# Order of work between and inside the feed-forwards of a two-layer encoder: when weights are split, finished blocks added, squares summed

## The chip, the cores and the metric

One NeuronCore of a Trainium2 chip runs the whole program. The metric is device microseconds from launch to end, the median of several executions. An engine is named as the profile names it: PE (TensorE, matrix products), PEld (its weight loads), DVE (VectorE), ACT (ScalarE), POOL (GpSimd) and SP (SyncE, which here only issues transfers).

## What is computed

The input x is 512 tokens of 1024 features in float32. There are two layers, and each is

```
x = x + 0.5 * swiglu(rms(x, ffn1_norm), ffn1_w)      # feed-forward, 2816 hidden columns
x = x + mixer(rms(x, mix_norm))                      # layer 0: windowed attention, layer 1: latent attention
x = x + 0.5 * swiglu(rms(x, ffn2_norm), ffn2_w)
swiglu(h, w) = (silu(h @ w_gate) * (h @ w_up)) @ w_down
```

and a last rms norm. So four feed-forwards run one after the other, numbered f = 0 to 3 here; mixers stand between 0 and 1 and between 2 and 3, and nothing stands between 1 and 2.

## The kernel before

**Numbers.** PE multiplies rounded float32 values. To keep precision each operand is split in two: ACT copies it into a rounded high part, DVE subtracts that from the original and leaves the low part. A product is then three matmuls (high by high, high by low, low by high). Every weight goes through ACT and then DVE before PE can use it; `high...` functions are ACT's half of a split and `low...` functions DVE's half.

**Units.** A feed-forward is 30 units, u = 0 to 29 (`ffn_units`, line 50): 22 "G" units (one gate and up tile of 128 hidden columns each) and 8 "D" units (blocks of the down projection, put in after unit 9 and after the second run of gates). A unit of 2 by 2 blocks is done with seven products instead of eight, in the way of Strassen and Winograd: weights are combined into sums, inputs are combined into sums, and the results are combined again. Product q of unit u is P_q(u) below: 12 matmuls of 256 columns. Unit 0 is done without this, as two plain tiles of 48 matmuls (`plain_tile`, line 1895). PE's order is in `ffn` at line 1922: in period u it runs P1(u), P2(u), P4(u-1), P6(u), P3(u-1), P5(u), P7(u). P4 and P6 add to a bank that holds an earlier product, so they wait until that has been copied out.

**Weights.** Each unit has six splits, called fills (`fill`, line 555): FA (1024 columns), FB, FC, FD, FE and FU (512 each). FB holds the sum called S2 and feeds P6, FE feeds P7, FU P5, FC P4, FD P3, and FA both P1 and P2. FU, FB and FD of one unit come out of one buffer, a chain of four: SP loads a first piece, and POOL adds three more pieces by accumulating transfers (`link`, line 775). Step 0 makes FU's data; when FU has been split, step 1 adds a piece and makes FB's; when FB has been split, step 2 makes FD's. FE comes from a single buffer with one added piece (`join`, line 790). FA and FC are loaded plain. POOL's order of issues is in `ffn` at line 798.

**Order on ACT and DVE.** Both run in program order (ACT: `ffn`, line 994; DVE: `ffn`, line 1465), and a wait of one item holds up all behind it. In period u ACT does: FU(u+1), copy of P1 (line 1005, "first copy"), FA(u+1), silu of the first half, FC(u), copy of P6 (line 1021), FB(u+1), FD(u), silu of the second half of u-1, copy of P7 (line 1042, "last copy"), FE(u+1). P4(u) in the next period waits for that last copy. DVE has the low halves in the same order, with the sums and products of results among them: addition with the last copy at line 1541, norm factor of the gate at line 1422. `fill_count` (line 74) gives each fill its place in this order; semaphores fill_hi and fill_lo are waited on by these counts, so the count and the two engines' orders must be the same.

**Combined units.** In units 3, 5, 7, 9, 14, 17, 19 and 21 (`combined`, line 169) the hidden columns just computed are combined into the inputs of the down projection as well: DVE makes four sums (line 1246 to 1254), and ACT and DVE split seven blocks of 256 columns (lines 904, 913, 1259, 1269).

**Between feed-forwards.** The output of what came before f = 1, 2, 3 (8 blocks of 128 features) is added to x in `pairs_out` (ACT line 954, DVE line 1340). Per block j, DVE first splits the weights of block n+j+3 (`low`), then adds block j to x (line 1351); ACT scales the new x (line 925), squares it (line 937), and per pair of blocks the split inputs and sums of the first products are made (`pair_split`, `pair_mix`). Fills FA, FU and FC of unit 0 stand at j = 6, at j = 7 and after the loop. Then `begin` makes FU(1), the last mixed inputs, the norm (POOL's power, line 773, and four small steps on DVE), FA(1), FB(1) and FE(1). For f = 0 the inputs come from transposes, and squares and sums alternate with the mixed inputs (lines 1075 and 1596). `sums` (line 1956) adds the squares over features on PE; `spread` (line 1968) puts the norm factor on all partitions.

**Transfers that the end of a feed-forward waits for.** In f = 0 and 2 SP loads rotary tables before it loads the first blocks of what follows, and waits for the last FE to be split (line 696); ACT's first `high` of those blocks stands in unit 29 (line 1008), DVE's at line 1499.

```python
                if part is not None:
                    sp.wait_ge(fill_lo, fill_count(f, FE, NU - 1))
                    sp.dma_start(tables[:, part * S:3 * S], consts[:, P + part * S:]).then_inc(t_in, 16)
```

## Time and profile before

| | us |
|---|---|
| median of 3 runs (lowest, highest) | 1857.53 (1855.23, 1859.74) |
| the profiled execution, its own time | 1855.27 |
| its span, first to last instruction | 1853.5 |
| PE busy | 1737.3 |
| DVE busy | 1417.2 |
| ACT busy | 954.8 |
| mean granted TensorE clock | 0.981 |

The profile is of one execution. A row of a timeline is: start in us, duration in us, engine, line of the kernel, operation, tile written, tiles read, shape, number of instructions merged, and in brackets the idle time of the engine before it with what ended it. The arrow points to what was waited for. PEclk is the TensorE clock granted, as a share of full speed.

### The profile page before, as it was taken

How to read it: one execution, taken by the hardware profiler on the slowest of the kernel's cores; microseconds unless marked ns; L12 is line 12 of the kernel's file. 1: busy time of each engine (PE TensorE's matmuls, PEld its weight loads, DVE VectorE, ACT ScalarE, POOL GpSimd, SP SyncE). 2: the span in 40 equal slices, each digit the busy share in tenths (PEclk: the TensorE clock that was granted, in tenths of full speed). 3: DMA queues.
4: the chain of work that ended last, by engine and by line, in shares of the span. 5: the costliest groups of instructions: out<-in, count | busy, mean ns of one | idle time of the engine just before them, and what ended most of it. 6: DMA issues, size and time to landing. Idle time of an engine off the chain costs nothing. (4 is left out here: it accounts for less than half of the span.)

```text
span 1853.5 us, 34651 instructions
## 1 busy us (share of the span) xinstructions
PE 1737.3 (94%) x12937; PEld 1626.4 (88%) x12937; DVE 1417.2 (76%) x2776; ACT 954.8 (52%) x1892; POOL 434.8 (23%) x495
## 2 busy tenths in 40 slices
PE   5999999999989999999799999999999889999997
PEld 4999999877879899998799999987867789999995
DVE  5788787667678878866778788766897568878788
ACT  4554554446555545544555455544565445555452
POOL 0333333111013333330133333300000033333320
PEclk7999999999989999999899999999999989999999
DMA  5899999533439999995399999945112389999971
GB/s 173 192 219 237 224 220 229 149 110 91 125 91 220 221 228 217 226 245 154 69 224 224 226 223 230 209 117 132 30 40 58 108 182 220 230 226 221 226 163 69
DMA packets 187076, 324.18 MB, mean 175 GB/s; under 512 B 24545, under 2 KB 58526, under 8 KB 186910
## 3 DMA queue, kind: packets, MB, share of 16 engines
q0 software_dynamic: 66816, 121.66, 38.5%
q1 hardware_dynamic: 118528, 198.55, 33.9%
q8 instruction: 105, 1.72, 0.4%
q10 hardware_dynamic: 1566, 1.74, 0.3%
q14 instruction: 61, 0.50, 0.1%
HBM read 315.33 MB, written 2.10 MB: 171 GB/s over the span
## 5 line engine op out<-in xcount | busy, mean ns | idle before, releaser
L1889 PE MATMUL bank<-h_all,w_all 128*128 128x256 f32 x2352 | 672.2, 286 | 45.0 <-ACT work L1042 34.0
L1890 PE MATMUL bank<-h_all,w_all 128*128 128x256 f32 x2352 | 668.2, 284 | 0.0
L1891 PE MATMUL bank<-h_all,w_all 128*128 128x256 f32 x2352 | 668.0, 284 | 0.0
L1889 PEld LDWEIGHTS bank<-h_all,w_all 128*128 128x128 f32 x2352 | 453.9, 193 | 52.4 <-issue 34.4
L1890 PEld LDWEIGHTS bank<-h_all,w_all 128*128 128x128 f32 x2352 | 454.1, 193 | 0.0
L1891 PEld LDWEIGHTS bank<-h_all,w_all 128*128 128x128 f32 x2352 | 453.9, 193 | 0.0
L787 POOL DMA_DIRECT2D work<-ffn_gu x252 | 221.6, 923 | 825.3 <-DVE w_all L1238 593.3
L901 ACT ACTIVATE w_all<-work 128x512 fp32r<-128x512 f32 x352 | 208.9, 623 | 345.6 <-DMA work<-ffn_gu 222.3
L1238 DVE TENSOR_TENSOR w_all<-work,w_all 128x512 fp32r<-128x512 f32 x352 | 238.9, 687 | 150.4 <-ACT w_all L901 149.6
L1238 DVE TENSOR_TENSOR w_all<-r_all,w_all 128x512 fp32r<-128x512 f32 (+1 forms) x356 | 308.2, 866 | 21.7 <-ACT w_all L901 16.9
L901 ACT ACTIVATE w_all<-r_all 128x512 fp32r<-128x512 f32 (+1 forms) x356 | 273.0, 769 | 73.3 <-PE bank L1891 71.9
L1889 PE MATMUL bank<-y_all,w_all 128*128 128x256 f32 x896 | 254.4, 284 | 11.8 <-DVE w_all L1238 11.2
L1890 PE MATMUL bank<-y_all,w_all 128*128 128x256 f32 x896 | 253.7, 283 | 0.0
L1891 PE MATMUL bank<-y_all,w_all 128*128 128x256 f32 x896 | 253.6, 283 | 0.0
L1889 PEld LDWEIGHTS bank<-y_all,w_all 128*128 128x128 f32 x896 | 172.0, 192 | 13.3 <-DVE w_all L1238 13.3
L1891 PEld LDWEIGHTS bank<-y_all,w_all 128*128 128x128 f32 x896 | 172.0, 192 | 0.0
L1890 PEld LDWEIGHTS bank<-y_all,w_all 128*128 128x128 f32 x896 | 172.0, 192 | 0.0
L992 ACT ACTIVATE work<-work 128x256 f32<-128x256 f32 x168 | 70.0, 417 | 142.1 <-DVE work L1422 141.8
L787 POOL DMA_DIRECT2D work<-ffn_d x96 | 87.1, 991 | 165.0 <-DVE w_all L1238 165.0
L1225 DVE TENSOR_TENSOR w_all<-x_f,w_all 128x1024 fp32r<-128x1024 f32 (+2 forms) x72 | 69.0, 959 | 61.4 <-ACT w_all L876 55.9
L1409 DVE SCALAR_TENSOR_TENSOR xT<-bank,xT 128x256 f32<-128x256 f32 x224 | 93.9, 419 | 22.9 <-PE bank L1891 21.6
L1842 PE MATMUL bank<-y_all,w_all 128*128 128x512 f32 x272 | 107.4, 395 | 1.3 <-DVE w_all L1225 1.3
(214 smaller groups left out, 2787.1 us busy)
## 6 DMA issues: line engine op xcount, KB each, us to landing
work<-ffn_gu POOLq DMA_DIRECT2D x252, 256.0 KB, 5.9
r_all<-ffn_gu SPq DMA_DIRECT2D x88, 512.0 KB, 5.2
r_all<-ffn_gu SPq DMA_DIRECT2D x172, 256.0 KB, 6.3
work<-ffn_d POOLq DMA_DIRECT2D x96, 256.0 KB, 6.1
work<-ffn_gu SPq DMA_DIRECT2D x88, 256.0 KB, 5.6
r_all<-ffn_gu POOLq DMA_DIRECT2D x84, 256.0 KB, 7.2
r_all<-ffn_d SPq DMA_DIRECT2D x64, 256.0 KB, 5.8
r_all<-ffn_d SPq DMA_DIRECT2D x32, 512.0 KB, 5.3
```

The costliest lines, as they stand in the source:

```text
L787: pool.dma_start(chain[g % CHAIN], unit_source(f, u, slice(part * S, (part + 1) * S)), accum_op=ALU.add).then_inc(chain_sum[g % CHAIN], 16)
L901: a.activation(hi, src, ACT.Copy).then_inc(fill_hi, 1)
L992: a.activation(buf, buf, ACT.Silu).then_inc(silu_done, 1)
L1225: last = v.tensor_tensor(w_lo[:, sl, 0:k, 0:m], w_raw[:, sl, 0:k, 0:m], w_hi[:, sl, 0:k, 0:m].bitcast(F32), ALU.subtract)
L1238: v.tensor_tensor(lo, src, hi.bitcast(F32), ALU.subtract).then_inc(fill_lo, 1)
L1409: return v.scalar_tensor_tensor(at, src, -0.5 if c < PAIRED else 0.5, at, ALU.mult, ALU.add)
L1842: t.matmul(b[:, :], wh, hi[:, c, :], start=c == 0, stop=False)
L1889: t.matmul(o, wh, xh, start=c == 0 and not on, stop=False, skip_group_check=on)
L1890: t.matmul(o, wh, xl, start=False, stop=False, skip_group_check=on)
L1891: last = t.matmul(o, wl, xh, start=False, stop=c == PAIRED - 1, skip_group_check=on)
```

## The change

Six things are reordered. No instruction is added or taken away, and no transfer changes its size.

1. FB(u) and FE(u) are split in period u and no longer in period u-1. FB(u) comes first in the period, FE(u) after the first copy on ACT and after the norm of the gate on DVE (for u > 1).
2. In period u the silu of the second half comes before FD(u) on ACT. On DVE the addition after the last copy (`finish`) moves to the start of the next period, ahead of FB. In the units of f = 3 that also transpose x, it thereby comes after those transposes.
3. POOL's loop is written in another order to match.
4. `pairs_out`: DVE adds block j to x first and then splits the weights of block n+j+4; fills FA, FU, FC of unit 0 move to j = 4, 5, 6, and FU(1) to the end of the loop. The inputs of the last pair are split and mixed at j = 7 and right behind it.
5. f = 0: all squares and their sums come before any mixed input.
6. f = 0: PE runs both plain tiles before `sums`, and P2(1) before `spread`.

In the diff, the functions `ffn` come in the order POOL, ACT, DVE, PE; `pairs_out` is DVE's, and ACT's is changed alike. `finish(f, u)` and `finish_late(f, u)` hold the additions that stood at the end of period u.

```diff
 def fill_count(f, kind, u):
     if u < 2:
-        at = {FA: 0, FU: 1, FC: 2}[kind] if u == 0 else {FU: 3, FA: 4, FB: 5, FE: 6, FC: 9, FD: 11}[kind]
-    elif u == NU - 1 and kind in (FC, FD):
-        at = 6 * NU - (5 if kind == FC else 4)
+        at = {FA: 0, FU: 1, FC: 2}[kind] if u == 0 else {FU: 3, FA: 4, FB: 5, FE: 6, FC: 9, FD: 10}[kind]
+    elif kind in (FU, FA):
+        at = (7 if kind == FU else 8) if u == 2 else 6 * u - (6 if kind == FU else 4)
     else:
-        at = 6 * u + {FU: -5, FA: -4, FB: -2, FE: 0, FC: 3, FD: 5}[kind]
+        at = 6 * u - 1 + {FB: 0, FE: 2, FC: 4, FD: 5}[kind]
+        if u == NU - 1 and kind != FB:
+            at -= 1 if kind == FE else 2
...
             def ffn(f, m):
-                for u in range(NU + 1):
+                for u in range(NU):
+                    if u > 0:
+                        link(f, u, 2)
                     link(f, u + 1, 1)
                     if u == 0:
                         power(m)
                     link(f, u + 2, 0)
                     join(f, u + 2)
-                    link(f, u + 1, 2)
...
             def ffn(f):
+                    if u > 1:
+                        high_fill(f, FB, u)
                     high_fill(f, FU, u + 1)
...
+                    if u > 1:
+                        high_fill(f, FE, u)
                     high_fill(f, FA, u + 1)
...
-                    high_fill(f, FB, u + 1)
+                    if before:
+                        silu(f, u - 1, 1)
                     high_fill(f, FD, u)
                     if u == NU - 1:
                         high(SEG_AT[f] + 1, end)
-                    if before:
-                        silu(f, u - 1, 1)
...
-                    high_fill(f, FE, u + 1)
...
             def pairs_out(n, f, factor, begun=0):
                 end = n + KD
+                if not begun:
+                    low(n + AHEAD, end)
                 for j in range(KD):
-                    if j >= begun:
-                        low(n + j + AHEAD, end)
-                    if j == KD - 2:
-                        low_fill(f, FA, 0)
-                    if j == KD - 1:
-                        low_fill(f, FU, 0)
                     b = product(n + j)
                     v.scalar_tensor_tensor(xT[:, PERM[j], :], b[:, :], factor, xT[:, PERM[j], :],
                                            ALU.mult, ALU.add).then_inc(evac_done, 1)
-                    if j >= 3 and j % 2 and j < KD - 1:
-                        q = (j - 3) // 2
-                        low_mixed(h_mix, combine_count(f, q, False), q)
+                    low(n + j + AHEAD + 1, end)
+                    if 4 <= j < 7:
+                        low_fill(f, (FA, FU, FC)[j - 4], 0)
                     if j >= 2 and j % 2 == 0:
-                        pair_split(f, j // 2 - 1)
-                        pair_mix(f, j // 2 - 1)
+                        low_mixed(h_mix, combine_count(f, j // 2 - 1, False), j // 2 - 1)
                     if j:
                         added(j == 1)
-                pair_split(f, PAIRED - 1)
+                    if j % 2:
+                        pair_split(f, j // 2)
+                        if j < KD - 1:
+                            pair_mix(f, j // 2)
                 added(False)
-                low_fill(f, FC, 0)
-                low_mixed(h_mix, combine_count(f, PAIRED - 2, False), PAIRED - 2)
                 pair_mix(f, PAIRED - 1)
+                low_fill(f, FU, 1)
...
             def ffn(f, m):
+                    if u > 1:
+                        finish(f, u - 1)
+                        low_fill(f, FB, u)
                     low_fill(f, FU, u + 1)
+                    if u > 1 and UNITS[u - 1][0] == "D":
+                        finish_late(f, u - 1)
...
+                    if u > 1:
+                        low_fill(f, FE, u)
                     low_fill(f, FA, u + 1)
...
-                    low_fill(f, FB, u + 1)
...
             for k in range(KD):
                 added(k == 0)
-                if k % 2:
-                    pair_mix(0, k // 2)
-                    if k < KD - 1:
-                        low_mixed(h_mix, combine_count(0, k // 2, False), k // 2)
...
             def ffn(f, m, ready):
                 plain_tile(f, False)
-                sums(m, KD)
+                if f > 0:
+                    sums(m, KD)
                 plain_tile(f, True)
                 if f > 0:
                     pe.wait_ge(evac_done, ready)
+                else:
+                    sums(m, KD)
                 product(f, 1, 1)
-                spread(m + 1)
-                for q in (2, 6, 5, 7):
+                if f > 0:
+                    spread(m + 1)
+                product(f, 2, 1)
+                if f == 0:
+                    spread(m + 1)
+                for q in (6, 5, 7):
                     product(f, q, 1)
```

## Rows read from the trace of the kernel before

**Rows 1.** Who PE waited for: us in total, times, longest.
```profile
PE bank L1889 <- ACT work L1042: 34.0, 30, 3.3
...
PE bank L1964 <- DVE acc L1286: 14.7, 1, 14.7
PE bank L1916 <- DVE y_all L1264: 13.4, 5, 4.8
```

**Rows 2.** Windows: units without a stall; all four feed-forwards from P1(1) on.
```profile
655.00:725.00 70.00, 70.00 (x586) 70.00 (x585) 53.12 (x102) 35.64 (x63) 23.55 (x27) 1.00 1.02 234
...
sum 1245.50, PE 1188.74 PEld 1179.75 DVE 985.30 ACT 653.08 POOL 388.68; mean PE 297.19 PEld 294.94 DVE 246.33 ACT 163.27 POOL 97.17
```

**Rows 3.** Windows: the way into f = 1, and the start of f = 0.
```profile
526.00:549.00 23.00, 16.23 (x106) 16.06 (x107) 15.84 (x27) 8.93 (x14) 4.11 (x4) 0.78 0.26 66
...
32.80:50.00 17.20, 6.51 (x30) 6.51 (x31) 13.10 (x24) 7.32 (x11) 4.14 (x4) 0.50 0.10 17
```

**Rows 4.** Timeline of PE, into f = 1: last block, P1(1), P7(1).
```profile
525.49 0.39 PE L1844 MATMUL bank<-y_all,w_all 128*128 128x512 f32 x1
...
548.87 0.28 PE L1889 MATMUL bank<-h_all,w_all 128*128 128x256 f32 x1
...
556.62 0.36 PE L1889 MATMUL bank<-h_all,w_all 128*128 128x256 f32 x1 [1.37 <-DVE w_all L1238]
```

**Rows 5.** Timeline of DVE, into f = 1: last block added, last pair split, FU(1).
```profile
533.49 0.68 DVE L1351 SCALAR_TENSOR_TENSOR xT<-bank,xT 128x512 f32<-128x512 f32 x1
...
536.78 0.42 DVE L1264 TENSOR_TENSOR y_all<-work,y_all 128x256 fp32r<-128x256 f32 x1
...
541.10 0.68 DVE L1238 TENSOR_TENSOR w_all<-work,w_all 128x512 fp32r<-128x512 f32 x1
```

**Rows 6.** Timeline of POOL, into f = 1: step 0 of unit 2, issued behind the power.
```profile
544.40 0.90 POOL L787 DMA_DIRECT2D work<-ffn_gu  x1
```

**Rows 7.** Timeline of ACT, into f = 1: FU(2) when step 0 has landed.
```profile
551.14 0.63 ACT L901 ACTIVATE w_all<-work 128x512 fp32r<-128x512 f32 x1 [1.01 <-DMA work<-ffn_gu]
```

**Rows 8.** Timeline of DVE: FU(1) of f = 2 and of f = 3.
```profile
910.75 0.68 DVE L1238 TENSOR_TENSOR w_all<-work,w_all 128x512 fp32r<-128x512 f32 x1
...
1488.77 0.69 DVE L1238 TENSOR_TENSOR w_all<-work,w_all 128x512 fp32r<-128x512 f32 x1
```

**Rows 9.** Timelines at f = 0: DVE's first split of mixed inputs; PE's sums and P7(1).
```profile
30.28 1.23 DVE L1269 TENSOR_TENSOR h_all<-work,h_all 128x1024 fp32r<-128x1024 f32 x1 [1.12 <-ACT h_all L913]
...
43.49 0.37 PE L1964 MATMUL bank<-ones,acc 128*128 128x1 f32 x1 [14.65 <-DVE acc L1286]
...
60.88 0.36 PE L1889 MATMUL bank<-h_all,w_all 128*128 128x256 f32 x1 [1.42 <-DVE w_all L1238]
```

**Rows 10.** Timelines, combined unit 7 of f = 1: ACT's FB and last copy, DVE, PE's P4(7).
```profile
622.57 1.15 ACT L901 ACTIVATE w_all<-work 128x512 fp32r<-128x512 f32 x2 [3.16 <-DMA work<-ffn_gu]
...
625.57 0.36 ACT L1042 ACTIVATE work<-bank 128x256 f32<-128x256 f32 x1
...
621.56 0.95 DVE L1259 TENSOR_TENSOR y_all<-work,y_all 128x768 fp32r<-128x768 f32 x1
...
626.08 0.36 PE L1889 MATMUL bank<-h_all,w_all 128*128 128x256 f32 x1 [1.50 <-ACT work L1042]
```

**Rows 11.** Timelines, unit 29 of f = 2: DVE's FE(29), its gate norm; ACT's first next block.
```profile
1212.44 0.69 DVE L1238 TENSOR_TENSOR w_all<-r_all,w_all 128x512 fp32r<-128x512 f32 x1
...
1215.52 0.42 DVE L1422 TENSOR_TENSOR work<-work,r_x 128x256 f32<-128x256 f32 x1
...
1218.45 0.85 ACT L876 ACTIVATE w_all<-x_f 128x768 fp32r<-128x768 f32 x1 [5.12 <-DMA x_f<-ffn_e]
```

**Rows 12.** The source view: joins (line 795) idle until; landing of joins, then of links (line 787).
```profile
  issue: 162.3, 86
...
DMA to landing us min/median/max: 4.8/6.9/9.8
...
DMA to landing us min/median/max: 3.5/6.0/10.9
```

More of the change, by code:

```diff
@@ L1077, in _ @@
                 squared(xT[:, PERM[j], :], j == 0)
-                if j % 2 and j < KD - 1:
-                    high_mixed(h_mix, combine_count(0, j // 2, False), j // 2)
             end = SEG_AT[1]
@@ L1342, in pairs_out @@
                 end = n + KD
+                if not begun:
+                    low(n + AHEAD, end)
                 for j in range(KD):
[L1344 to L1349 removed]
                     b = product(n + j)
```

69 lines of the change are left out of this document (42 added, 27 removed).

## The prediction

> **What bounds the kernel.** I read who PE waited for first. PE is busy for 1737.3 of 1853.5 us, so the end is set by PE's own work and by its stalls, and only a stall taken away moves it. Of the stalls, the largest single one in number is the last copy on ACT, 34.0 us in 30 waits; 14.7 us is one wait for the sums of squares at the start; 13.4 us is for the inputs of the plain tiles [rows 1]. Then windows. In 70 us without a stall PE starts 586 matmuls, one per 0.1195 us, so that a product (12) takes 1.43 us and a period of seven 10.04 us. From P1(1) to the end each of the four feed-forwards is 203 products or 291 us; together 1166 us, while they took 1245.5 us [rows 2]. So 79 us are stalls inside, beside those on the ways in. On the way into f = 1 PE is busy for 16.2 of 23 us, at 0.78 of its clock, and DVE for 15.8: neither is full, which is the sign of a chain in which each waits for the other [rows 3].
>
> **Part 4, the ways in (f = 1, 2, 3).** The last block before f = 1 leaves PE at 525.9, P1(1) starts at 548.87 and P7(1) at 556.62 [rows 4]. What lies between is 96 matmuls of the plain tiles (11.5 us) and the sums (0.5), so P1(1) could stand at 537.9. It doesn't, because block 7 is added to x only at 533.49, 7.6 us after PE had it: DVE stands in front of it with FA and FU of unit 0, which wait for ACT, which waits for DVE's block before. From that add to the last split of the pair is 3.7 us, and from there to the end of the split FU(1) another 4.6, at 541.8 [rows 5]. With the add first, block 7 is added at 526.0. The pair is split at 529.7, before the first tile's last quarter (525.9 and 4.3), and FU(1), now ahead of the last mixed split of 1.2 us that stood before it and of FC, is done near 532.4: 9.4 earlier. FU(1) is the start of what follows: POOL issues step 1 of unit 1, then the power, then step 0 of unit 2 at 544.40 [rows 6]; that lands and lets ACT do FU(2) at 551.14 [rows 7], and the first copy, which P6(1) needs, stands behind FU(2). All of this moves along by 9.4 with unchanged lengths. PE is ahead of it (P2(1) ends near 541.3, FU(2) comes at 541.8), so the late thing is then step 0 of unit 2, and P6(1) waits 1.6 us for it. I take **-9.4** for f = 1. Bounds: 11.0 (P1(1) alone would move so much) and 4.0, if DVE is so far behind at j = 7 that only half is had.
>
> For f = 3 the same: FU(1) was done at 1489.5 [rows 8], the last block leaves PE at 1472.4 (the same distance of 6.4 us gives 1478.9), **-10.5**. For f = 2 a block is 18 matmuls of 512 columns, near 4.1 us, and DVE's work on one (a split, an add, half a pair) is near 4.3, so DVE is about 4 us late at block 7. FU(1), done at 911.4 before, comes at 902.5: **-8.9**. SP's and POOL's first loads of the next feed-forward are not behind any of this. Low and high splits of blocks n+4 to n+7 come at most one add (0.68) later for PE, which needs them three blocks later: nothing. If that cover were gone, it would be 0.7 for each of 5 blocks.
>
> **Parts 5 and 6, f = 0.** Sums came at 43.49 after an idle time of 14.65 us, since each round had a mixed input, in which DVE waited 1.12 for ACT [rows 9]. Seven adds back to back at 0.79 each from 26.95 end at 32.4, and PE meanwhile does the second tile, to 34.5. But the four mixed inputs now come after: for each DVE three sums (1.6), ACT's half (1.1), DVE's half (1.2), 3.9 in all with the waits, from 34.1 to 50.1 with the norm between. P6(1) needs all four, and ACT's first copy is behind the last of them, near 51. PE thus idles from about 41 to 51, and its restart is at half the clock as the first one was (0.50 from 32.8 to 50 [rows 3]). The silu and the copies of unit 1 then set P7(1), near 57.2 in place of 60.88 [rows 9]: **-3.7**. Bounds: -6 and +2 (if a slow restart pushes P6(1) past those copies). The Trainium skill, TensorE: Matmul & The Clock Gate, HAM oscillation, says the same of a wait as this row, that work after it starts cold; were the restart warm, P6 and P5 would end 2.9 earlier and P7(1) would still wait for the copy, so the sum would not change.
>
> **Parts 1 and 2, inside.** In unit 7 ACT sat idle 3.16 us until FB(8) had landed, and behind it stood FD(7), the silu, a mixed input and the last copy, at 625.57. P4(7) waited 1.50 for that [rows 10]. With FB behind the copy, a plain unit's P4 no longer waits. A combined unit keeps DVE's own chain: its split of 621.56 ends at 622.5, then the norm (0.4), silu (0.5), FD (0.5), mixed (0.9), copy (0.4): 625.2 less overlaps of a few tenths, 0.8 us sooner. Of the 34.0 us some 5.6 belong to unit 29 (below). The other 28.4, in 26 waits, lose 0.8 each, 20.8. Against it, FB is now split by DVE after that late copy, and P6 wants it 4.3 us into the period; after a combined unit I get 4.7 to 5.1, a wait of 0.3 in 24 places, 7. **-14**. Bounds: -34, all of that row and nothing given back, and 0, all given back.
>
> **POOL.** The sequence of issues is the same as before, only the loop is written differently: step 2, step 1, step 0, join. The times differ. The join waited for nothing that a semaphore tells for 162.3 us in 86 cases, and landings take 6.0 us for a link and 6.9 for a join [rows 12]; the spacing fits three such transfers in flight at most, the fourth issued when one lands. Steps 2 and 1 are now 0.6 us apart instead of 3 to 5, so step 0 has to wait for the join of the unit before, near 5.8 us into a period. It lands 2.4 into the next, where FU wants it at 1.1. There are 1.9 us left before the first copy makes P6 late: nothing, unless landings grow. **The 16 DMA engines** are 1.02 busy at 234 GB/s at full speed [rows 2], and one unit is nine pieces of 256 KB, 10.1 us at that rate; three units are loaded ahead, so 27 in 294 us need 272. I exclude a bound by bytes.
>
> **The end of f = 0 and 2.** Here the change costs. SP's loads of the next blocks wait for FE(29), which was split at 1212.44 and now comes after the gate's norm, which ends at 1215.9 [rows 11]: 3.5 us later. ACT already sat idle 5.12 us for such a load at 1218.45, with the silu, FC(29) and the P6 copy behind it, so P7(29) and P4(29) are 3.5 later. And silu, FD(29), the next block and the last copy are now in a row after the silu: 1.4 more. **+4.9** each, 9.8. For f = 1 and 3, whose loads are early, 1.5 each: **+3**. Bounds: +6 and +16.
>
> **Sum.** -9.4 -10.5 -8.9 -3.7 -14 +9.8 +3 = -33.7 us. Against the profiled execution, 1855.3, that is 1821.6. The median of the runs stands 2.3 above it, 1857.5, and for the median I say 1824. A difference under 0.2% (3.7 us) can't be told from none here.
>
> **Rivals.**
> (a) DVE is the bound. It is busy 53.1 of 70 us [rows 2], but in a combined unit its list is about 11 us against a period of 10. Then what P4 gains P6 gives back (0 for -14), and the ways in give half (-16 for -32.5). With +12.8 that is -3, or 1854; with the ways in full, -20, or 1838. For it: the 0.3 above is a difference of large numbers. Against it: each other unit leaves 2 us to catch up. Chance 0.19 for something from 1838 to 1852.
> (b) Slower: POOL's three places. From FB(u) to FU(u+3) there is now a chain of three landings (step 2, join, step 0), 19 us of landing and 1 of issue, in 20.1 + 1.4. If bunched transfers land 15% later, 22 us, the excess is 1.5 in each two periods, over 116 periods 87 us, less -34 with the stalls inside: about +40, or 1897. It decides once the three take over 20.7. Maxima of 9.8 and 10.9 are in the rows [rows 12], but in crowds at a start. For the crowding: the Trainium skill, DMA: Bandwidth & Descriptors, Issuing engines are not separate DMA queues, says that all queues share the same 16 engines and interleave. By that, spacing within a period changes no total, and rows 2 agree, with 1.02 busy and PE still full. Chance 0.07.
> (c) No change, losses at the end of a feed-forward and the gains cancelling: 0.04.
> (d) As computed, 1808 to 1838: 0.66. More than that, stalls inside nearly all gone: 0.04.
> That gives faster 0.89, same 0.04, slower 0.07. The range for 8 in 10 takes (d) and the better half of (a): 1804 to 1848.
>
> **What would show it.** Into f = 1, block 7 is added within 1 us of PE's end of it, and P1(1) starts within 14 us of it. The wait for the last copy falls under 20 us. POOL's idle before its links moves to step 0. At the end of f = 0 and 2, ACT waits over 7 us for the next block. I am wrong if PE waits for FB in every period, if FU waits over 3 us for its landing in steady units, or if DVE has no idle time left before f = 1.

## The result: 0.85% slower, and the profile after

The changed kernel takes 1874.07 us (median of 4 runs, 1865.85 to 1876.89) against 1856.38 us before (4 runs). The ratio is 1.0085, with a 95% interval from 1.0059 to 1.0111. Forecast were 1824 us and 0.982.

| | before | after |
|---|---|---|
| the profiled execution, its own time, us | 1855.27 | 1865.85 |
| span, us | 1853.5 | 1864.0 |
| PE, DVE, ACT busy, us | 1737.3, 1417.2, 954.8 | 1745.0, 1420.5, 953.5 |
| mean granted TensorE clock | 0.981 | 0.984 |

The profiled execution was the shortest of the four. So the sum of the prediction is judged against a difference of 10.6 us in span; what the other three took on top has no trace.

The next table cuts both spans at starts and ends of products on PE. "Inside" is P7(1) to P1(28), "end" is P1(28) to the end of P3(29), "way" is from there to the next P7(1).

| stretch, us | before | after | difference | forecast |
|---|---|---|---|---|
| start to P7(1) of f = 0 | 60.9 | 55.5 | -5.4 | -3.7 |
| ways into f = 1, 2, 3 | 194.1, 66.3, 277.3 | 194.5, 57.1, 275.7 | +0.4, -9.2, -1.6 | -9.4, -8.9, -10.5 |
| inside f = 0, 1, 2, 3 | 274.8, 277.6, 275.5, 278.3 | 282.6, 279.6, 279.9, 281.6 | +17.4 together | -14 |
| ends of f = 0, 1, 2, 3 | 26.8, 25.1, 25.8, 25.7 | 32.1, 24.1, 28.7, 31.0 | +5.3, -1.0, +2.9, +5.3 | +4.9, +1.5, +4.9, +1.5 |
| after the last P3(29) | 45.2 | 41.5 | -3.7 | 0 |

Two rows are far off: the ways into f = 1 and 3, and inside. The waits of PE after the change, to be set beside [rows 1] (us in total, times, longest):

```profile
PE bank L1911 <- ACT work L1052: 30.2, 27, 2.9
PE bank L1911 <- DVE w_all L1245: 27.3, 33, 9.6
PE bank L1938 <- DVE y_all L1271: 22.6, 8, 6.4
...
PE bank L1911 <- ACT work L1014: 4.5, 7, 2.5
```

The wait for the last copy (now line 1052) fell only from 34.0 to 30.2. Waits for splits of weights (line 1245), which cost 14.8 us before, take 27.3 (9.6 of it is one wait at the start of f = 0, below), those of the plain tiles for their inputs (line 1271) 22.6 in place of 13.4, and PE now waits for the first copy (line 1014).

**The way into f = 1.** Timelines of ACT, of DVE and of PE (start, us, engine, line; in brackets idle time before it):

```profile
527.78 1.06 ACT L904 ACTIVATE w_all<-r_all 128x1024 fp32r<-128x1024 f32 x1 [9.03 <-PE bank L1866]
...
533.23 0.63 ACT L904 ACTIVATE w_all<-work 128x512 fp32r<-128x512 f32 x1 [2.30 <-PE bank L1866]
```

```profile
520.76 0.68 DVE L1354 SCALAR_TENSOR_TENSOR xT<-bank,xT 128x512 f32<-128x512 f32 x1
...
531.76 0.68 DVE L1354 SCALAR_TENSOR_TENSOR xT<-bank,xT 128x512 f32<-128x512 f32 x1
...
538.18 0.68 DVE L1354 SCALAR_TENSOR_TENSOR xT<-bank,xT 128x512 f32<-128x512 f32 x1
...
541.13 0.69 DVE L1354 SCALAR_TENSOR_TENSOR xT<-bank,xT 128x512 f32<-128x512 f32 x1
```

```profile
544.99 0.56 PE L1938 MATMUL bank<-h_all,w_all 128*128 128x256 f32 x1 [6.43 <-DVE y_all L1271]
```

Blocks 4 to 7 are added at 520.76, 531.76, 538.18 and 541.13. PE had the last of them at 533.13, so block 7 is added 8.0 us late, where it was 7.6 before [rows 4, 5]. Between blocks 4 and 5 stand 11 us: ACT waits 9.03 us to split FA of unit 0, and what it waits for is a matmul of the block products. FA goes into slot 0 of `w_all`, FU into slot 1, FC into slot 2. The eight blocks lie in slots 2, 3, 0, 1, 2, 3, 0, 1 for f = 1 and 3, and in 0, 1, 2, 3, 0, 1, 2, 3 for f = 2 (`slot`, `high_fill`). So at j = 4 FA waits for PE's block 6, and at j = 5 FU for block 7; at j = 6 ACT had split FA before the change without a wait:

```profile
525.61 1.04 ACT L901 ACTIVATE w_all<-r_all 128x1024 fp32r<-128x1024 f32 x1
```

In f = 2, where FA and FU wait for blocks 4 and 5, the way is 9.2 us shorter, near the 8.9 forecast.

**Inside.** Stalls of PE between P7(1) and P1(28), by the product that they precede, summed over four feed-forwards (distance of two starts less 12 times 0.1197 us, 183 distances in each):

| us before | P1 | P2 | P3 | P4 | P5 | P6 | P7 | all |
|---|---|---|---|---|---|---|---|---|
| kernel before | 0.6 | 0.4 | 2.2 | 32.7 | 0.6 | 17.9 | 0.4 | 54.8 |
| after | 1.1 | 5.6 | 4.6 | 26.9 | 0.4 | 31.2 | 2.6 | 72.3 |

P4 gained 5.8 and everything else lost 23. And P4 gained in plain units only: in the 32 combined units its stalls are 27.3 us before and 26.7 after, in all others 5.4 before and 0.2 after. Of P6's 31.2 us, 19.0 stand in the units that follow a combined one and 6.9 in the combined ones. Two of ACT's waits, first before and then after the change (us in total, times, longest):

```profile
ACT work L992 <- DVE work L1422: 141.8, 148, 3.2
```

```profile
ACT work L999 <- DVE work L1438: 322.3, 146, 5.4
```

ACT's waits for landings of the links' data fell from 337.4 us to 163.7, and those for DVE's norm of the gate rose by 180.5: the idle time changed its cause and did not go. Combined unit 7 of f = 1 after the change, to be set beside [rows 10]; timelines of ACT, DVE and PE:

```profile
631.74 0.42 ACT L999 ACTIVATE work<-work 128x256 f32<-128x256 f32 x1 [4.07 <-DVE work L1438]
632.06 0.61 ACT L904 ACTIVATE w_all<-work 128x512 fp32r<-128x512 f32 x1
632.58 1.04 ACT L916 ACTIVATE y_all<-work 128x1024 fp32r<-128x1024 f32 x1
633.53 0.36 ACT L1052 ACTIVATE work<-bank 128x256 f32<-128x256 f32 x1
```

```profile
631.29 0.42 DVE L1438 TENSOR_TENSOR work<-work,r_x 128x256 f32<-128x256 f32 x1
632.71 0.69 DVE L1245 TENSOR_TENSOR w_all<-work,w_all 128x512 fp32r<-128x512 f32 x1 [1.00 <-ACT w_all L904]
```

```profile
634.04 0.36 PE L1911 MATMUL bank<-h_all,w_all 128*128 128x256 f32 x1 [1.25 <-ACT work L1052]
```

ACT no longer waits for the landing of FB. It waits 4.07 us for DVE's norm of the gate instead, then come silu, FD, mixed inputs and at last the copy for P4(7), which stalls 1.25 us where it stalled 1.50. And DVE now stands still for 1.00 us between its norm and its half of FD, because on ACT the silu is ahead of FD.

**Ends.** ACT's first block of what follows in f = 0 and f = 2, to be set beside the 5.12 us of [rows 11]:

```profile
358.78 0.84 ACT L879 ACTIVATE w_all<-x_f 128x768 fp32r<-128x768 f32 x1 [8.10 <-DMA x_f<-ffn_e]
...
1224.45 0.84 ACT L879 ACTIVATE w_all<-x_f 128x768 fp32r<-128x768 f32 x1 [6.31 <-DMA x_f<-ffn_e]
```

In f = 3 it is another thing, two transposes of x (line 1420) that now stand ahead of DVE's addition and of FB(29). Timelines of DVE and PE:

```profile
1803.83 2.50 DVE L1420 STREAM_TRANSPOSE x_f<-xT 32x1024 f32<-32x1024 f32 x2
1806.36 0.42 DVE L1487 TENSOR_TENSOR work<-bank,work 128x256 f32<-128x256 f32 x1
```

```profile
1807.43 0.38 PE L1911 MATMUL bank<-h_all,w_all 128*128 128x256 f32 x1 [1.39 <-DVE w_all L1245]
...
1819.62 0.55 PE L1911 MATMUL bank<-h_all,w_all 128*128 128x256 f32 x1 [1.70 <-DVE work L1487]
```

PE loses 5.3 us there, but the kernel does not: from P1(29) to the end DVE is the later engine (its last transposes end at 1840.73, and 23.3 us of final norm follow the last transposes in both kernels), so that end and tail together cost 1.6.

**The start of f = 0.** A window while P6(1) waits, and PE's wait:

```profile
41.47:50.46 8.99, 0.00 (x1) 0.02 (x1) 6.54 (x11) 4.04 (x7) 0.00 (x0) 0.50 0.30 50
```

```profile
50.46 0.57 PE L1911 MATMUL bank<-h_all,w_all 128*128 128x256 f32 x1 [9.58 <-DVE w_all L1245]
```

PE idles for 9 us, with a granted clock of 0.50, as the prediction had it (41 to 51), and P7(1) comes at 55.5.

### The profile page after: what moved, and what is told of

The parts are those of the page before. It is cut to its first block and busy times, and to the rows that moved or that the text cites. A ratio compares the mean times of both kernels' runs of the same rounds, so it can differ in the third digit from the quotient of the medians.

```text
span 1864.0 us, 34651 instructions
## 1 busy us (share of the span) xinstructions
PE 1745.0 (94%) x12937; PEld 1627.1 (87%) x12937; DVE 1420.5 (76%) x2776; ACT 953.5 (51%) x1892; POOL 436.5 (23%) x495
## 5 line engine op out<-in xcount | busy, mean ns | idle before, releaser
L1911 PE MATMUL bank<-h_all,w_all 128*128 128x256 f32 x2352 | 676.9, 288 | 60.8 <-ACT work L1052 30.2
L904 ACT ACTIVATE w_all<-work 128x512 fp32r<-128x512 f32 x352 | 215.7, 624 | 213.8 <-DMA work<-ffn_gu 102.3
L1245 DVE TENSOR_TENSOR w_all<-r_all,w_all 128x512 fp32r<-128x512 f32 (+1 forms) x356 | 299.1, 864 | 12.8 <-ACT w_all L904 12.1
L904 ACT ACTIVATE w_all<-r_all 128x512 fp32r<-128x512 f32 (+1 forms) x356 | 264.3, 767 | 48.9 <-PE bank L1913 32.6
L1864 PE MATMUL bank<-y_all,w_all 128*128 128x512 f32 x272 | 107.1, 394 | 0.0
L1866 PE MATMUL bank<-y_all,w_all 128*128 128x512 f32 x272 | 106.1, 390 | 0.0
```

The lines of the kernel that those rows point to most:

```text
L904: a.activation(hi, src, ACT.Copy).then_inc(fill_hi, 1)
L1245: v.tensor_tensor(lo, src, hi.bitcast(F32), ALU.subtract).then_inc(fill_lo, 1)
L1864: t.matmul(b[:, :], wh, hi[:, c, :], start=c == 0, stop=False)
L1866: last = t.matmul(b[:, :], wl, hi[:, c, :], start=False, stop=c == k - 1)
L1911: t.matmul(o, wh, xh, start=c == 0 and not on, stop=False, skip_group_check=on)
```

## The experiments

Two bases are used: the changed kernel (runs a_...), and the kernel before with parts 4 to 6 alone (b_...); a_part1 and the runs p1_... are the latter with part 1 added. Stalls are those inside, as in the table above; for the changed kernel 72.3 us. The expectations count about 11.9 us more in each such total (5.8 at P5 and 5.8 at P6, which the starts in the traces don't bear out). It is the same amount in every run, so differences between runs stand, and a bound of theirs is compared after taking 11.9 off a total and 5.8 off P6.

| run | median, us | ratio to before, 95% interval | stalls inside | span of the profile |
|---|---|---|---|---|
| a_slots | 1862.67 | 1.0023 (1.0001 to 1.0044) | 88.5 | 1862.8 |
| a_fd_first | 1857.28 | 0.9998 (0.9978 to 1.0018) | 68.0 | 1855.9 |
| a_tables_late | 1868.11 | 1.0037 (1.0015 to 1.0059) | 90.0 | 1872.5 |
| a_fd_copy1 | 1856.79 | 0.9991 (0.9968 to 1.0014) | 62.8 | 1845.8 |
| a_nojoin | 1868.40 | 1.0044 (1.0029 to 1.0059) | 70.4 | 1867.0 |
| a_pool_sum | 1895.56 | 1.0197 (1.0162 to 1.0231) | 100.4 | 1897.7 |
| b_outer | 1838.86 | 0.9892 (0.9856 to 0.9928) | 46.0 | 1832.8 |
| b_outer_slots | 1828.56 | 0.9826 (0.9788 to 0.9864) | 54.6 | 1827.2 |
| b_copy_early | 1828.10 | 0.9822 (0.9791 to 0.9853) | 58.0 | 1825.6 |
| b_pool_sum | 1836.39 | 0.9897 (0.9866 to 0.9927) | 61.6 | 1831.7 |
| b_best | 1835.05 | 0.9877 (0.9857 to 0.9898) | 67.6 | 1833.8 |
| a_part1 | 1857.57 | 1.0002 (0.9979 to 1.0024) | 82.5 | 1853.5 |
| b_light | 1814.28 | 0.9772 (0.9739 to 0.9804) | 42.1 | 1810.4 |
| p1_light | 1823.45 | 0.9824 (0.9779 to 0.9870) | 45.3 | 1816.0 |
| p1_nostep2 | 1819.46 | 0.9790 (0.9759 to 0.9820) | 46.2 | 1820.3 |
| b_nostep2 | 1801.46 | 0.9688 (0.9658 to 0.9718) | 30.7 | 1799.5 |
| b_copy_tables | 1823.82 | 0.9806 (0.9781 to 0.9832) | 56.9 | 1822.1 |

How far one profile can be trusted: f = 0 is the same code in the changed kernel, a_slots and (up to its end) a_tables_late, and took 282.6, 285.5 and 285.5 us inside. So a few us of one stretch are not told apart by single profiles; medians and ratios decide where they disagree. a_nojoin, b_light, p1_light and the two runs without step 2 leave work out, so their outputs are not those of the program: they measure, and are no versions to use.

**1. Slots (a_slots).** FILL_AT is 6 for f = 1 and 3, and 4 for f = 2; ACT's side is edited alike.

```diff
-                    if 4 <= j < 7:
-                        low_fill(f, (FA, FU, FC)[j - 4], 0)
+                    if FILL_AT[f] <= j < FILL_AT[f] + 3:
+                        low_fill(f, (FA, FU, FC)[j - FILL_AT[f]], 0)
...
+                if FILL_AT[f] == 6:
+                    low_fill(f, FC, 0)
```

> The changed kernel, but on the ways into f = 1 and 3 fills FA, FU and FC of unit 0 stand at j = 6, at j = 7 and after the loop again (behind the addition of the block), as the slots of w_all that they need come free there; the way into f = 2 keeps j = 4, 5, 6. Theory 1 (slots): in f = 1 and 3 FA at j = 4 has to wait for PE's block 6 and FU at j = 5 for block 7, and the additions of blocks 5 to 7 stand behind them. Then the way into f = 1 (end of P3(29) to P7(1), 194.5 us in the changed kernel) falls to 185 to 187 and into f = 3 (275.7) to 266 to 269, the rest stays, the span falls from 1864 to 1846 to 1849. Rival (DVE simply has too much work on these ways, wherever the fills stand): each way gets at most 2 shorter, span 1860 or more.

The ways came out as expected: 184.3 us into f = 1 and 266.5 into f = 3, so 10.2 and 9.2 shorter. DVE's addition of block 7, and the window from PE's end of block 7 to P1(1), in this run:

```profile
536.58 0.69 DVE L1357 SCALAR_TENSOR_TENSOR xT<-bank,xT 128x512 f32<-128x512 f32 x1 [0.38 <-PE bank L1871]
```

```profile
536.20:548.78 12.58, 12.58 (x107) 12.54 (x105) 10.00 (x20) 7.23 (x11) 4.12 (x4) 1.00 0.20 37
```

DVE waits for PE and not the other way round. From the end of block 7 to P1(1) PE is busy throughout, for 12.6 us in place of 23, and the clock stays at 1.00, where it was 0.78 [rows 3]. But the span fell by 1.2 only, to 1862.8, which is what the rival had (1860 or more), since stalls inside grew by 16 in this profile. By the medians the gain is 11.4. The mechanism is shown by the ways; the 15 to 18 us expected to the end of the kernel were not had.

**2. FD ahead of the silu (a_fd_first).**

```diff
-                    if before:
-                        silu(f, u - 1, 1)
                     high_fill(f, FD, u)
                     if u == NU - 1:
                         high(SEG_AT[f] + 1, end)
+                    if before:
+                        silu(f, u - 1, 1)
```

> The changed kernel, but in each period ACT splits FD(u) before the silu of the second half, as before the change. Theory 2 (a round trip): with the silu first DVE stands still 1.00 us in every period between the norm of the gate and its half of FD, and in combined units, where DVE is the bound, that pushes the last copy and all that follows. Then DVE's idle time in front of fills from work for ACT (176 us) falls by 50 to 100, the stalls of P4 in combined units (1.41 each) fall to 0.4 to 0.9, the stalls between P7(1) and P1(28), 84 us in all, to 60 to 72, and the span to 1842 to 1852. Rival (FB at the head of the period is what costs, or POOL's landings): under 4 us in all, stalls in front of P6 unchanged.

P4's stalls fell from 26.9 to 13.3, and the one that recurs in combined units (5, 7 and 19 above all) from 1.41 to 0.89, as expected; P6's grew from 31.2 to 39.3, and neither the stalls inside (expected 48 to 60 by this count) nor the span (1842 to 1852) got where theory 2 had them. The timeline of DVE in unit 7 shows where the 1.00 us went, and ACT's shows who is late now:

```profile
628.13 0.68 DVE L1245 TENSOR_TENSOR w_all<-work,w_all 128x512 fp32r<-128x512 f32 x1
629.65 1.23 DVE L1276 TENSOR_TENSOR y_all<-work,y_all 128x1024 fp32r<-128x1024 f32 x1 [0.83 <-ACT y_all L916]
```

```profile
625.48 0.63 ACT L904 ACTIVATE w_all<-work 128x512 fp32r<-128x512 f32 x1 [1.30 <-DMA work<-ffn_gu]
```

FD follows the norm without a wait, but then DVE waits 0.83 us for the mixed inputs, and ACT waits 1.30 for the landing of FD's data. The median fell by 16.8 and the span by 8.1, of which f = 3's end and tail are 3.7 and the stalls inside 4.3. Theory 2 is half right: the round trip is real, its removal is partly given back.

**3. Parts 4 to 6 alone (b_outer, b_outer_slots).**

> The kernel before with parts 4, 5 and 6 alone (additions first on the ways in, squares ahead of sums at f = 0), order inside the units as before. If the parts add up: f = 0 starts 5.4 us earlier, the ways give 0 (f = 1), 9.2 (f = 2), 1.6 (f = 3), the stalls inside and the ends are those of before: span 1836 to 1840 against 1853.5. If the gains on the ways hang on the order inside the units (what POOL and SP issue first, and so the landings), the sum is under 10 us: 1844 or more.

> The kernel before with parts 4, 5 and 6 and with the fills of unit 0 where their slots are free (j = 6, 7, end for f = 1 and 3, j = 4, 5, 6 for f = 2). By theory 1 and the sum of the run before: 16 us more than that, span 1819 to 1824. By the rival of theory 1 no better than 1835.

b_outer is 1.1% faster than before, a little more than the parts summed to (span 1832.8 against 1836 to 1840). With the fills where their slots are free it is 1.7% faster. The ways are 7.8 and 7.7 us shorter than in b_outer, but of these 15.5 the median shows 10.3 and the span 5.6 (1827.2, outside the expected 1819 to 1824): P4's stalls inside rose from 26.2 to 33.3. So parts 4 to 6 are a gain even as they stand in the change, and the loss lies in parts 1 to 3.

**4. SP's wait ahead of the tables (a_tables_late).**

```diff
-                if part is not None:
-                    sp.wait_ge(fill_lo, fill_count(f, FE, NU - 1))
-                    sp.dma_start(tables[:, part * S:3 * S], consts[:, P + part * S:]).then_inc(t_in, 16)
                 for j in range(KD):
+                    if part is not None and j == SLOTS:
+                        sp.wait_ge(fill_lo, fill_count(f, FE, NU - 1))
+                        sp.dma_start(tables[:, part * S:3 * S], consts[:, P + part * S:]).then_inc(t_in, 16)
```

> The changed kernel, but at the end of f = 0 and f = 2 SP issues the loads of the next four blocks ahead of its wait for FE(29) and the load of the tables. Theory 3 (the step of the prediction on the ends): FE(29) is split 3.5 us later than before the change, and behind that wait stand the loads of the next blocks, for which ACT waits. Then the end of f = 0 (P1(28) to the end of P3(29), 32.1 us in the changed kernel) falls to 25 to 27 and that of f = 2 (28.7) to 25 to 26.5, the span by 8 to 10 us. Rival (the order silu, FD, next block inside unit 29 is what lengthens the ends): they fall by under 2 us each, the span by under 4.

The end of f = 0 fell from 32.1 to 24.1 and that of f = 2 from 28.7 to 25.0. ACT's first block in f = 0 no longer waits for a landing:

```profile
355.15 0.85 ACT L879 ACTIVATE w_all<-x_f 128x768 fp32r<-128x768 f32 x1 [0.60 <-PE bank L1913]
```

Theory 3 holds for the stretch. The span of this profile is longer all the same (stalls inside 90.0); the median is 6.0 lower, with intervals that just touch (1.0015 to 1.0059, and 1.0059 to 1.0111 for the changed kernel).

**5. The two copies moved on ACT (a_fd_copy1, b_copy_early).** In the first the first copy goes ahead of FU(u+1), in the second the last copy ahead of the mixed inputs:

```diff
+                    if gate and u > 1:
+                        act.wait_ge(prod_done, product_count(f, 1, u))
+                        act.wait_ge(e_2, at)
+                        a.activation(s_1, b[:, 0:HN], ACT.Copy).then_inc(e_1, 1)
                     high_fill(f, FU, u + 1)
```

```diff
+                    if gate:
+                        act.wait_ge(prod_done, product_count(f, 7, u))
+                        act.wait_ge(e_5, at)
+                        a.activation(u_3, b[:, 0:HN], ACT.Copy).then_inc(e_7, 1)
                     if q is not None:
                         high_mixed(y_mix, combine_count(f, q, True), q % PAIRED)
```

> The run with FD ahead of the silu, and ACT's first copy ahead of FU(u+1) too (from u = 2 on). Theory 4 (a queue on ACT): with FB(u) and FU(u+1) both at the head of the period, the first copy, which P6(u) needs, stands behind FU(u+1), whose data land late; PE waited 14.2 us for it in 17 places. Then these waits go, the stalls in front of P6 (45 us) fall to 31 to 35, the span (1855.9) to 1843 to 1848. Rival (DVE's fills are late anyway, so that P6 waits for FB in the same places): P6's stalls stay over 40 and the span over 1852.

> The kernel before with parts 4 to 6 and the fills where their slots are free, and ACT's last copy ahead of the split of the mixed inputs in combined units (1.04 us of work of ACT moved behind it). If the last copy is only late by what stands ahead of it on ACT, the stalls of P4 in combined units fall by up to 1.04 each: P4's 33 us inside to 12 to 18, the span from 1827 to 1808 to 1814. Rival (DVE's own list bounds a combined unit, so that what P4 gains P6 or the next unit loses): total of the stalls inside falls by under 7 us, span 1820 or more.

(At the old places the same lines are taken out.) Both moved the stall that they were aimed at, and neither moved the time. Waits of PE for copies, first a_fd_first, then a_fd_copy1 (its last copy is line 1056):

```profile
PE bank L1911 <- ACT work L1014: 14.2, 17, 1.8
PE bank L1911 <- ACT work L1052: 12.6, 17, 1.7
```

```profile
PE bank L1915 <- ACT work L1056: 21.2, 20, 1.7
```

The 14.2 us for the first copy are gone, P6's stalls fell from 39.3 to 21.9, and P4's rose from 13.3 to 22.6. In b_copy_early P4's fell from 33.3 to 12.7 and P6's rose from 17.3 to 34.9. The medians went from 1857.3 to 1856.8 and from 1828.6 to 1828.1. (The profile of a_fd_copy1, 1845.8, was the shortest of its ten runs; by it alone theory 4 would look right.) This is what rival (a) of the prediction said: what P4 gains P6 gives back.

**6. Fewer transfers on POOL (a_nojoin).** The accumulating transfer for FE is left out.

> The changed kernel without POOL's adding transfer of the buffer of FE (its sum lacks one piece; 116 transfers of 256 KB fewer, a quarter of POOL's). If the stalls in front of P6 come from landings (POOL has at most three transfers in flight and the links stand bunched), the irregular ones go: P6 37 us to 18 to 24, DVE and ACT wait less for links, span 1845 to 1852. If they come from the order on DVE and ACT alone, P6's stalls stay over 32 and the span over 1858.

P6's stalls stayed (32.1 for 31.2), with ACT's waits for the links' data down from 102.3 us to these:

```profile
ACT w_all L902 <- DMA work<-ffn_gu: 77.7, 63, 4.8
```

The median is 5.7 lower, with intervals that just touch. The mere number of POOL's transfers is not what costs most.

**7. A sum on POOL (a_pool_sum, b_pool_sum), and with the tables' edit (b_best).**

```diff
+            def first_sum(f, q):
...
+                g.tensor_tensor(x_sum[:, 0:2, :], x[:, 2:0:-1, :], x[:, 3:4, :].to_broadcast([P, 2, HN]), ALU.subtract)
...
                     link(f, u + 1, 1)
+                    if u in COMBINED:
+                        first_sum(f, COMBINED[u])
                     link(f, u + 2, 0)
```

> The changed kernel, with the first of the four sums of a combined unit (0.69 us on DVE) made by POOL, between the issues of step 1 and step 0. Theory 5 (DVE bounds the combined units): a cycle of a combined and the next plain unit is 14 products, 20.1 us, but DVE is busy for 20.5 us in it; the cycle took 21.4 us before the change and 22.2 after it, the difference being DVE's own waits. Then 0.6 less work of DVE shortens each such cycle by 0.4 to 0.6: stalls inside 84 to 68 to 76, median (1874) down by 8 to 16 us. Rival (the waits for landings and the order on ACT bound the cycle): no more than 3 us.

> The same edit on the kernel before with parts 4 to 6 and the fills where their slots are free (median 1828.6, stalls inside 66.5 us). Theory 5: cycle from 21.5 to 20.9 or less, P4's stalls 33 to 20 to 25 with no growth at P6, median 1814 to 1820. Rival (as for the run before): 1825 or more.

> The run with the sum on POOL, and SP's loads of the next four blocks ahead of its wait for FE(29) and the tables. If theories 3 and 5 hold and add up: 3 to 4 us under the run with the sum alone (ends 26.9 and 25.9 to 24.1 and 25.0), median 1811 to 1816. If a faster end is given back on the way in or inside: no difference from it.

a_pool_sum is 21.5 us slower than the changed kernel, b_pool_sum and b_best are 7.8 and 6.5 slower than b_outer_slots (the last with intervals that overlap). DVE was not relieved. Groups of instructions by form, in b_outer_slots and in b_pool_sum (busy us, mean ns):

```profile
L1243 DVE TENSOR_TENSOR w_all<-r_all,w_all 128x1024 fp32r<-128x1024 f32 x120 | 146.3, 1219 | 9.4 <-ACT w_all L902 9.2
```

```profile
L1253 DVE TENSOR_TENSOR w_all<-r_all,w_all 128x1024 fp32r<-128x1024 f32 x120 | 178.8, 1490 | 8.4 <-ACT w_all L912 8.2
```

```profile
L804 POOL TENSOR_TENSOR work<-work 128x512 f32<-128x512 f32 x32 | 45.9, 1434 | 0.0
```

DVE's half of FA grew by 32.5 us over the kernel. In the trace 29 of its 120 instructions overlap a sum of POOL (1.43 us) and take 2.34 us in the mean, the other 91 take 1.22: 1.1 us more for each that overlaps, while the sum that left DVE was 0.69. On POOL the sum also waits for its inputs ahead of step 0, which was not measured by itself. So the test said nothing on theory 5, and the runs of the next part replace it. (The 20.5 us in the expectation is PE's mean busy time of a cycle; DVE's is 18.3, see the rows of the next part.)

**8. Which part, and by what (a_part1, b_light, p1_light, p1_nostep2, b_nostep2).** a_part1 is b_outer_slots with part 1 alone, and with the order of POOL's loop that belongs to it (part 3), so the two are not told apart:

> The kernel before with parts 4 to 6, free slots, and of the changes inside the units part 1 alone (FB(u) and FE(u) split in period u, POOL's order with it); the silu and DVE's addition after the last copy stand as before the change. It splits the loss inside: against the same kernel without part 1 (span 1827, stalls inside 66.5). Theory 6 (part 1 costs: FB and FU stand together at the head of a period, where ACT and DVE are late after the last copy, and DVE waits for ACT for each): stalls inside 76 to 84, with the later ends of f = 0 and 2 a span of 1840 to 1848. Rival (the silu and the moved addition were the cost): stalls inside 64 to 70, span 1831 to 1836, which is the ends alone.

It took 82.5 us of stalls inside, 27.9 more than b_outer_slots, and a median 29.0 higher, more than either theory had: part 1 by itself costs 1.8% of the kernel. Parts 1 and 2 together (a_slots) stand at 1.0023, part 1 at 1.0002, so the silu and the moved addition cost about 0.2%, where the two intervals overlap. That is less than a_fd_first gave for the silu alone in the changed kernel (from 1.0085 to 0.9998, 0.9%). No run explains the difference, so the price of part 2 is known only as 0.2 to 0.9%.

Then two remedies on both sides of part 1. "light" does four operations of DVE in combined units on 8 columns only, "nostep2" drops step 2 of the links:

```diff
-                        mix(q % 2, k, 0)
+                        mix(q % 2, k, 0, 8)
...
-                        normed_silu(f, u - 1, 0)
+                        normed_silu(f, u - 1, 0, 8 if u in COMBINED else HN)
```

```diff
-                    if u > 0:
-                        link(f, u, 2)
...
-    return 16 * (3 * CHAIN_TURN[f, u] + steps)
+    return 16 * (2 * CHAIN_TURN[f, u] + min(steps, 2))
```

> The kernel before with parts 4 to 6 and free slots (median 1828.6, stalls inside 66.5 us), where in combined units four of DVE's operations (the first sum, two norms of the gate, one of the silu) work on 8 columns only, so that sums and norms are left out there for the other columns: about 1.6 us less for DVE in each combined unit. Theory 5 (DVE's list bounds them): the cycle of a combined and a plain unit falls from 21.5 to 20.2 to 20.5 us, the stalls inside to 35 to 48, the span to 1796 to 1810. Rival (landings, or the order on ACT): stalls inside over 58, span over 1819.

> The same relief of DVE on the kernel with part 1 added (median 1857.6, stalls inside 94.4 us, cycle 22.2). If part 1 costs because DVE, already full, gets waits of its own at the head of a period, the cycle falls by 1.2 to 1.6 and the stalls inside to 50 to 66. If part 1 costs through landings, they stay over 75.

> The kernel with part 1, without step 2 of POOL's links (the data of FD lack a piece and are ready when FB's are; 116 transfers fewer). Landings as the cause of part 1's cost: ACT no longer waits for FD's data, the last copy is earlier, stalls inside 94.4 to under 78, median 1857.6 to under 1842. DVE or the order as the cause: stalls inside over 88, median over 1852.

> The kernel before with parts 4 to 6 and free slots (median 1828.6, stalls inside 66.5 us) without step 2 of POOL's links (FD's data lack a piece; 116 transfers fewer). If the late landing of step 2 is what part 1 brings, it costs next to nothing here: stalls inside 58 to 66, median 1820 to 1828, against a fall of 38 us for the same edit with part 1. If landings cost the same in both orders, the stalls inside fall under 45 and the median under 1808.

| ratio to before | as it is | light | no step 2 |
|---|---|---|---|
| without part 1 | 0.9826 | 0.9772 | 0.9688 |
| with part 1 | 1.0002 | 0.9824 | 0.9790 |
| cost of part 1 | 1.8% | 0.5% | 1.0% |

By the intervals of the ratios each cost is uncertain by 0.4 to 0.6 points (an estimate from their widths): with "light" it can't be told from none, and the fall from 1.8% to 1.0% is only just clear.

The cycle of a combined and the next plain unit (P4(3) to P4(5), P4(5) to P4(7), P4(7) to P4(9) and P4(19) to P4(21) of each feed-forward, 16 windows), summed; with the mean busy time of each engine. In turn: before, after, b_outer_slots, b_light, b_nostep2, a_part1, p1_light, p1_nostep2.

```profile
sum 342.37, PE 327.93 PEld 324.80 DVE 293.11 ACT 196.44 POOL 112.46; mean PE 20.50 PEld 20.30 DVE 18.32 ACT 12.28 POOL 7.03
```

```profile
sum 355.32, PE 334.11 PEld 325.15 DVE 295.13 ACT 196.19 POOL 112.38; mean PE 20.88 PEld 20.32 DVE 18.45 ACT 12.26 POOL 7.02
```

```profile
sum 343.73, PE 327.55 PEld 324.93 DVE 294.05 ACT 197.18 POOL 112.48; mean PE 20.47 PEld 20.31 DVE 18.38 ACT 12.32 POOL 7.03
```

```profile
sum 338.84, PE 326.34 PEld 323.40 DVE 271.87 ACT 195.75 POOL 112.63; mean PE 20.40 PEld 20.21 DVE 16.99 ACT 12.23 POOL 7.04
```

```profile
sum 335.53, PE 326.65 PEld 323.49 DVE 291.50 ACT 195.47 POOL 85.32; mean PE 20.42 PEld 20.22 DVE 18.22 ACT 12.22 POOL 5.33
```

```profile
sum 355.10, PE 334.14 PEld 325.07 DVE 294.31 ACT 200.09 POOL 112.32; mean PE 20.88 PEld 20.32 DVE 18.39 ACT 12.51 POOL 7.02
```

```profile
sum 334.98, PE 327.14 PEld 323.67 DVE 269.16 ACT 197.44 POOL 112.37; mean PE 20.45 PEld 20.23 DVE 16.82 ACT 12.34 POOL 7.02
```

```profile
sum 343.60, PE 331.98 PEld 324.47 DVE 292.58 ACT 195.78 POOL 85.50; mean PE 20.75 PEld 20.28 DVE 18.29 ACT 12.24 POOL 5.34
```

A cycle is 14 products, 20.1 us. It takes 21.4 us before (342.37 / 16) and 22.2 after, with the same 18.3 to 18.5 us of work on DVE in it. DVE has thus 1.7 us to spare over the 20.1 and spends them, and more, on waits for ACT. With part 1, 1.6 us less work of DVE shortens the cycle by 1.26, four fifths of it: there DVE's row of work and waits is most of the bound. Without part 1, 1.4 us less shorten it by 0.31: there it mostly isn't, and the missing step 2 gives more (0.51). In the order with part 1 the missing step 2 gives 0.72. Neither theory alone fits; the cost of part 1 is smaller when one of the two is taken away, DVE's fullness above all. ACT's waits for landings in a_part1 and in p1_nostep2:

```profile
ACT w_all L905 <- DMA work<-ffn_gu: 207.3, 150, 4.8
...
ACT w_all L905 <- DMA work<-ffn_d: 115.6, 66, 5.0
```

```profile
ACT w_all L903 <- DMA work<-ffn_gu: 71.5, 41, 4.6
ACT w_all L903 <- DMA work<-ffn_d: 41.9, 25, 3.2
```

With step 2 they come to 322.9 us, without it to 113.4. But in b_outer_slots, without part 1, they are 339.0 us in 127 waits against these 322.9 in 216: part 1 makes them more frequent and not longer in sum, so these totals don't show a share of the landings in its cost; the 1.8% that becomes 1.0% is the evidence for it.

Left open: whether step 2 costs by its own landing, for which FD waits, or because it keeps the other links of POOL from going out. For step 2 as something that only part 1 brings the expectation of b_nostep2 had 0.6 to 8.6 us, and 27 came, so step 2 costs in the order of before too.

**9. The best version (b_copy_tables).**

> The kernel before with parts 4 to 6, free slots, the last copy ahead of the mixed inputs and SP's loads of the next blocks ahead of the tables. Ends of f = 0 and 2 shorter by 2.8 and 0.9 us as in the run on the changed kernel, the rest as in the run with the copy alone (1828.1): median 1823 to 1827; if a faster end is given back, 1827 to 1830.

1823.8 us, 1.9% under the kernel before by the ratio, and 2.7% under the changed one by the medians. The ends of f = 0 and 2 are 24.1 and 24.5 us. From b_outer_slots its interval does not tell it apart.

## Why the prediction was wrong, by its own steps

- **Part 4, f = 2: right.** -8.9 forecast, -9.2 measured.
- **Part 4, f = 1 and 3: wrong,** +0.4 and -1.6 in place of -9.4 and -10.5. The failed step is "with the add first, block 7 is added at 526.0". It took the additions as free once they were first in their own j, and did not price fills FA and FU, which had moved from j = 6 and 7 to j = 4 and 5. Their slots come free with blocks 6 and 7 there. a_slots puts them back and gets 10.2 and 9.2. The trace of before did not show such a wait, as ACT split FA there at j = 6 (525.61) without idle time in front; where the slot comes free was in the kernel's lines.
- **Parts 5 and 6: right,** -5.4 against -3.7, with PE's pause and its clock as written.
- **Parts 1 and 2, inside: wrong in sign,** +17.4 for -14. The failed step is the last copy of a combined unit "0.8 us sooner", from which "0.8 each, 20.8". It took the copy as late by ACT's wait for FB only. P4 gained 5.8, of it 0.6 in combined units (27.3 to 26.7): there ACT now waits for DVE's norm in its place (4.07 us in unit 7). The step "a wait of 0.3 in 24 places, 7" for P6 came to 13.3, and waits in front of P2, P3 and P7 that no step had add 9.8 (5.6, 4.6 and 2.6 for 0.4, 2.2 and 0.4). What the runs showed in their place: a wait moved from one product to another is not a wait gained (a_fd_copy1, b_copy_early), and part 1, with FB and FU both at the head of a period, costs 1.8%; with 1.6 us less work for DVE in a cycle it costs 0.5%, so that the lack of room on DVE is the larger part of its cause. How the rest divides is open. And the silu ahead of FD makes DVE stand still for 1.00 us, a wait added by part 2 that the working passed over although it named the order.
- **Rival (a)** had this mechanism ("what P4 gains P6 gives back"), with 0.19 and 1838 to 1852. It put the gift back at zero and not beyond, and did not count the waits of DVE in a combined unit.
- **Rival (b)**, POOL's chain of three landings, was priced at +40 with 0.07 (its terms, 87 less 34, give 53). Its threshold of 20.7 us was not tested. But without step 2 part 1 costs 1.0% in place of 1.8%, so landings, or the order of POOL's issues, are part of the cost, and they were held at nothing in the sum. The Trainium skill, DMA: Bandwidth & Descriptors, Issuing engines are not separate DMA queues, says that transfers run on the same 16 DMA engines and interleave, whichever engine started them. No run here tests that by itself. The share of the DMA engines, 0.95 and 0.94 in the last two of the 16 cycles before the change and 0.91 and 0.88 after, shows only that they were no fuller after it; what ACT waited for was the landing of single transfers.
- **Ends: right in sum and cause** for f = 0 and 2, +8.2 of +9.8, and a_tables_late takes them away. The end of f = 1 came out at -1.0 for +1.5. Not foreseen was the transposes' place in f = 3, and that the tail, set by DVE, hides what they cost PE.
- **Its own signs.** Block 7 was added 8.0 us after PE had it (within 1 was forecast), P1(1) came 23.8 us after it (within 14), and the wait for the last copy was 30.2 us (under 20). ACT's wait of over 7 us for the next block came in f = 0 (8.10) and not quite in f = 2 (6.31).
- **A slip of arithmetic** in its first paragraph, 4 times 291 given as 1166 and not 1164, enters no term of the sum.

The errors add up: ways +18.4, inside +31.4, f = 0 -1.7, ends and tail -3.8, together 44.3, and -33.7 + 44.3 is the 10.6 that came.

## What to carry to other kernels

When a step is moved forward in a queue, ask first what it waits for at its new place, slot by slot, for every way on which the code runs: the same line was worth 9 us in one of three places and next to nothing in two. Before pricing a wait that goes, look for the second engine that is full in the same units; two runs that moved a copy took 17 and 21 us off one product, gave 9 and 18 back at another and left the median where it was. Splitting data later to be rid of an idle time on ACT cost 1.8% here, and the idle time only changed its cause, from landings to DVE's norm.

## What was not expected of the hardware

- **POOL and DVE at once.** A sum of 128x512 float32 on POOL takes 1434 ns in 32 cases, and each of the 29 subtractions of 128x1024 on DVE that overlap one in b_pool_sum takes 2.34 us, where the other 91 take 1.22. Work taken from DVE to POOL cost more DVE time (32.5 us in all) than it freed (32 sums of 0.69, 22.1 us).
- **Spread.** Executions of one kernel differed by less without step 2, in the few there are, and no run says why: 1798.7 to 1801.9 us in four of b_nostep2, 1818.7 to 1822.1 in four of p1_nostep2. The other kernels with four or five executions spread over 5.4 us (b_best) to 20.1 us (p1_light).
- **The clock's part.** On the way into f = 1 the granted clock was 0.78 over the 23 us from block 7 to P1(1) before, and 1.00 over the same stretch of 12.6 us in a_slots, where PE did not pause. Over the whole kernel it moved little: 0.981 before, 0.984 after, 0.989 in a_part1, whose time is that of before.
